# Moving two start addresses in SBUF: normed activations to 192 modulo 256, weight pieces by 128 bytes

## The reference

```python
# first block
mod = silu(c) @ w_ada[l] + b_ada[l]                     # 2048 -> 12288
h = rmsnorm(x, g_mix[l]) * (1.0 + sc1) + sh1
x = x + gt1 * hybrid_mixer(h, w_in, ..., w_out)         # pool, attention and LRU branches
h = rmsnorm(x, g_ffn[l]) * (1.0 + sc2) + sh2
x = x + gt2 * ((silu(causal_dwconv(h @ w_gate)) * (h @ w_up)) @ w_down)   # 2048 -> 5632 -> 2048
# second block, two layers
h = rmsnorm_2(x, norm_mix[l]);  proj = h @ w_in[l]      # three kinds of attention
x = x + mix @ w_o[l]
h = rmsnorm_2(x, norm_mlp[l])
u = relu(h @ w_up[l]);  x = x + (u * u) @ w_down[l]     # 2048 -> 8192 -> 2048
```

## The kernel before, in words

| tile | role in the matmuls | mod 256 | mod 512 |
|---|---|---|---|
| xT | none | 128 | 128 |
| h_hl (hi and lo, 16384 bytes apart) | moving | 128 | 128 |
| raw/w_lo and w_hi, slot 0 | stationary | 128 | 128 |
| slot 1 | stationary | 0 | 256 |
| slot 2 | stationary | 128 | 384 |
| slot 3 | stationary | 0 | 0 |
| sq, ident, ones, cols, mod | small matmuls, columns | 128 | 128 |
| act_hi, act_lo | moving | 192 | 448 |

## Time and profile before

### The profile page before, as it was taken

How to read it: one execution, slowest core, us unless ns; L and a number is a source line. 1 busy time by engine, 2 the same in 40 slices (tenths; PEclk the granted TensorE clock), 3 DMA queues, 4 the chain that set the end, 5 groups by cost and what they waited for, 6 DMA issues and landing times.

```text
span 3693.4 us, 59737 instructions
## 1 busy us (share of the span) xinstructions
PE 3377.6 (91%) x25150; PEld 3178.7 (86%) x25150; DVE 2343.3 (63%) x2598; ACT 1431.1 (39%) x1408; POOL 158.2 (4%) x292
## 2 busy tenths in 40 slices
PE   3497996999999988999999999998898999999997
PEld 3486886999999978877899999998787889999997
DVE  6777778756555566557655665666556756566655
ACT  1133433343443434344444443443343534344343
POOL 2111111100000000002000000000001000000000
PEclk9998998999999999999999999999999999999999
DMA  9687766755555543334455555554334455555553
GB/s 321 225 274 268 270 235 244 249 184 190 183 184 190 182 159 116 125 100 140 160 189 187 193 184 191 188 187 148 115 107 128 143 171 184 191 188 187 192 186 122
DMA packets 320586, 681.63 MB, mean 185 GB/s; under 512 B 14608, under 2 KB 21460, under 8 KB 320004
## 3 DMA queue, kind: packets, MB, share of 16 engines
q1 hardware_dynamic: 283440, 560.11, 45.4%
q0 software_dynamic: 31232, 109.07, 8.5%
q10 hardware_dynamic: 5780, 10.53, 0.9%
HBM read 677.47 MB, written 7.94 MB: 186 GB/s over the span
## 4 chain that ended last, share of the span: by engine, by line
PE 80%; DVE 11%; DMA 5%; issue 3%; ACT 2%; ACTq 0%; POOL 0%; POOLq 0%; DVEq 0%; SPq 0%
PE G L598 47%; PE Dn L598 31%; DMA ada_raw<-in_w_ada 3%; DVE ada_acc L1164 2%; DVE w_lo L1063 2%; PE Dn L601 1%; DMA raw<-in_w_in 1%; DVE sq L1099 1%; ACT w_hi L1792 1%; DVE negmax L1391 0%; DVE xT L1418 0%; DVE xT L1629 0%; DVE h_hl L1637 0%; DVE sq L1615 0%; DVE s_sb L1388 0%
## 5 line engine op out<-in xcount | busy, mean ns | idle before, releaser
L598 PE MATMUL G<-h_hl,w_hi 128*128 128x256 f32 (+1 forms) x9472 | 2109.2, 312 | 62.5 <-DVE w_lo L1063 21.2
L598 PEld LDWEIGHTS G<-h_hl,w_hi 128*128 128x128 f32 x9472 | 1567.6, 194 | 169.2 <-issue 32.4
L598 PE MATMUL G<-h_hl,w_lo 128*128 128x256 f32 x5760 | 1641.8, 285 | 0.0
L1063 DVE TENSOR_TENSOR w_lo<-raw,w_hi 128x2048 fp32r<-128x2048 f32 (+2 forms) x536 | 1218.7, 2274 | 599.5 <-ACT w_hi L1792 596.8
L1792 ACT CAST w_hi<-raw 128x2048 fp32r<-128x2048 f32 (+2 forms) x536 | 1015.5, 1896 | 1419.7 <-DMA raw<-in_w_up 395.6
L598 PEld LDWEIGHTS G<-h_hl,w_lo 128*128 128x128 f32 x5760 | 1110.8, 193 | 0.0
L598 PE MATMUL Dn<-act_hi,w_hi 128*128 128x256 f32 x2752 | 763.5, 277 | 7.3 <-DVE act_lo L1500 7.3
L598 PE MATMUL Dn<-act_lo,w_hi 128*128 128x256 f32 x2752 | 762.5, 277 | 0.0
L598 PE MATMUL Dn<-act_hi,w_lo 128*128 128x256 f32 x2752 | 762.5, 277 | 0.0
L598 PEld LDWEIGHTS Dn<-act_hi,w_hi 128*128 128x128 f32 x2752 | 517.4, 188 | 9.1 <-DVE act_lo L1500 7.9
L598 PEld LDWEIGHTS Dn<-act_hi,w_lo 128*128 128x128 f32 x2752 | 517.6, 188 | 0.0
(11 more groups left out here) (193 smaller groups left out, 1607.7 us busy)
## 6 DMA issues: line engine op xcount, KB each, us to landing
raw<-in_w_up SPq DMA_DIRECT2D x128, 1024.0 KB, 5.4
raw<-in_w_down SPq DMA_DIRECT2D x128, 1024.0 KB, 5.0
ada_raw<-in_w_ada POOLq DMA_DIRECT2D x192, 512.0 KB, 5.7
raw<-in_w_in SPq DMA_DIRECT2D x88, 1024.0 KB, 5.2
raw<-in_w_ffn_gate SPq DMA_DIRECT2D x44, 1024.0 KB, 5.0
raw<-in_w_ffn_up SPq DMA_DIRECT2D x44, 1024.0 KB, 5.0
raw<-in_w_ffn_down SPq DMA_DIRECT2D x44, 1024.0 KB, 5.0
raw<-in_w_o SPq DMA_DIRECT2D x32, 1024.0 KB, 5.0
```

What stands on the lines that cost most here:

```text
L598: return nc.tensor.matmul(o, lhsT, rhs, start=start, stop=stop, skip_group_check=True)
L1063: v.tensor_tensor(w_lo[j][:, 0:m], raw[j][:, 0:PIECE_K * n], w_hi[j][:, 0:m], ALU.subtract).then_inc(lo_done, 1)
```

## The change

The two 64-byte tiles `rs_v` and `rs_y` (scratch of the reciprocal root) are declared earlier: one between `xT` and `h_hl`, one between `h_hl` and the weight slots. No instruction is added, removed or reordered.

```diff
         xT = sb("xT", [P, KT, T])
+        rs_v = sb("rs_v", [P, 16])
         h_hl = sb("h_hl", [P, 2, KT, T], F32R)
         h_hi, h_lo = h_hl[:, 0, :, :], h_hl[:, 1, :, :]
+        rs_y = sb("rs_y", [P, 16])
         over = ExitStack()
         raw = [sb(f"raw{i}", [P, PIECE_K * 520], F32, over) for i in range(SLOTS)]
...
         amod = sb("amod", [P, 2, KT])
-        rs_v = sb("rs_v", [P, 16])
-        rs_y = sb("rs_y", [P, 16])
         rs_z = sb("rs_z", [P, 16])
```

## The result

The changed kernel takes 3661.3 us, the median of four runs (3657.5 to 3667.2); the kernel before, beside it on the same chip, 3694.2. The ratio of the two is 0.9909, with a 95% interval of 0.9894 to 0.9924: faster by 33 us or 0.9%, where the forecast said 83.6 us and a time between 3585 and 3645.

The account below looks back on a forecast made before the run. The matmul stream alone was taken to bound the feed-forward loops, its pace set by tile start addresses. 27.1 + 6.8 + 24.0 + 25.7 = 83.6 us off 3694.6 gave 3611.0 us, range 3585 to 3645.

Parts of the forecast that it names:

- (a): First feed-forward part, 11 groups: all 12 pieces at 5.44 us, group 65.28 instead of 67.75 us, saving 27.1 us.
- (b): Down slot 0 in the second block, 32 groups: from 5.65 to 5.44 us, saving 6.8 us.
- (c): Up in the second block, pairs of 512 and 256 columns: from 351.7 to 340 ns each, saving 24.0 us.
- Rival 1: Residues modulo 512 decide; a quarter of all pieces stay at 117.7 ns; 56.7 us saved, 3638 us; chance 0.15.
- (0,192): Stationary residue 0, moving 192, modulo 256: slot 0 of gate and up after the change, forecast at 113.3 ns.
- Rival 3: Second block's up: the pair does not follow its parts' pace; 59.6 us saved, 3635 us; chance 0.17.
- (d): Projections and attention of all three layers, 6960 matmuls on h_hl: saving between 10.4 and 41.1 us, middle 25.7 taken.
- (e): Some 900 small matmuls through ident, ones and sq, residues 128 to 0: 0 taken, 6 us to either side.
- Rival 2: No effect: G, its accumulation or h_hl's place slows gate, so 5.75 and 5.70 only exchange slots; 3694 us; chance 0.08.
- Rival 4: Slower: h at 192 locks every slot to gate's 119.8 ns, pairs 359.4; 3710 us; chance 0.05.

Follow-up runs that it names:

- The second execution of the changed kernel: The changed kernel run again with nothing altered, beside two other versions on the same chip: 3661.6 us, ratio 0.9908 to the kernel before.
- the probe: Whole computation left out; matmul streams alone over eight stationary and eight moving tile residues, all combinations: 113.3 to 120.0 ns a matmul, pairs 346.7 to 353.3.
- the split version of before: Kernel before, h_hl still at 128, each 512-column matmul of the second block's up projection written as two of 256: 3705.8 us, ratio 1.003.
- the all-192 kernel: Changed kernel's h and act at 192, all eight weight slots at 0: with pairs 3683.9 us; with pairs split 3642.5 us, six runs 3620.4 to 3661.0.

## Why the prediction was right and wrong, step by step

**What bounds the kernel, and that addresses matter:** right. Not an instruction was added, TensorE stayed busy in all but 2.5 us of each loop, and the loops shortened with the pace alone.

**(a) First feed-forward part, 27.1 us:** 22.7 measured. The size of a group, 65.28 us, came exactly. 4.5 us were counted for gate and up of groups 0 and 1 and 1.6 came. 13 of these 16 pieces run at 113 ns and TensorE's busy time falls by 3.5 us, but its idle time grows from 8.1 to 10.1 us: this part is not bound by the matmuls alone, and I counted it as if it were. In the loop 1.5 us less came than the groups give. Its last down group waits 2.5 us for `act_lo` in both kernels; after this wait the granted clock is 0.74 and 0.91 in the two stretches of 5 us from 1320 us on, where it was 1.00 before, that is some 1.7 us of time lost once. The second execution of the changed kernel has 3.4 us at the lower clock in this loop too, the version with h alone moved has none, so it comes and goes.

**(b) Down slot 0 in the second block, 6.8 us:** right, 5.65 to 5.46 us, 32 x 0.19 = 6.1, which the loops hold together with the loss of (c). The reading that this slot is slow by its history holds: with h alone moved it has the residues of before and runs at 113.3 ns in the first block's loop. Rival 1 is refuted by the profile after (gate slot 1, with the difference 192 modulo 512, runs at 113.3 ns). But the mechanism was only half told. In the second block of that same version slots 0 to 2 are slow, so the weights' shift was needed there. And the probe shows that the entry chooses between two paces at one pair of residues, where I had taken (0,192) for fast "in a usual group"; it was fast in all the loops of the changed kernel, which no row assured.

**(c) Pairs, 24.0 us:** this is the step that failed, and the largest miss: -3 us instead (32 x -0.09), 27 off. I argued that the present pair costs three present matmuls (351.7 and 3 x 117.2) and would follow its parts to 340. But 117.2 is only 351.7 / 3 and stands in no row. The parts at that address are gate's 118.7 and 119.8, which give 357.6 (3 x 119.2), as the split version of before then showed. So the pair was already faster than its parts, and the earlier trace rows said so. What the runs show in place of this step: the pair has a pace of its own for each difference. The probe has it at 353.3 at 192, its slowest. Rival 3, with 0.17, was the case. Only with the pair split does the forecast's 21.76 us a group come, by another edit.

**(d) Projections and attention, 25.7 us:** 9.5 measured, just under the lower end of 10.4, but not for the reason from which that end was worked out. The stream did get nearly as fast as the middle supposed. Taken over the matmuls that follow one another directly at the full clock, the mean distance of starts in these stages falls from 119.2 to 116.0 ns, stretches at 113.3 mixed with stretches at 117.7, and 3.2 x 6960 is 22 us. What failed is that the waits and the clock were put at nothing beyond this: TensorE's idle time in these stages grows from 134 to 141 us, and its time at the lower clock from 129 to 142 us, 11 us more of it busy and so some 5 us lost. In the second execution mixer 1's projections were 7 us shorter and the later stages of (d) longer by as much; idle time (142 us), time at the lower clock (143) and the 9.5 us below before came out alike. Why faster matmuls meet the lower clock more often was not looked into.

**(e) Small matmuls, 0:** not measured by itself; nothing in the differences asks for more. VectorE and ScalarE (2344.0 and 1432.7 us busy) are unchanged within 2 us, and DMA went from 186 to 192 GB/s in the first loop without becoming a bound, as reckoned.

In sum: 83.6, less 4.4 in (a), less 28.1 in (b) and (c), which together gave 2.7 of 30.8, less 16.2 in (d), leaves the 34.9 us of the stages. The step that failed first is (c), the pair priced by its parts; the second is (d), where faster matmuls were to cost nothing in waits and clock. The sign was right, and the saving at the upper end of the range was too large: 3645 held rival 3 alone (3635) but not rival 3 together with the lower end of (d), 3651, and the shortfall of (a) on top. Rival 2 falls: gate is not at 5.75 and 5.70. The rule in the Trainium skill, SBUF — State Buffer, section "SBUF: two separate sides", that the other engine ports never wait for anyone may be true of engines against each other; of TensorE's own two reads the probe shows 113.3 to 120.0 ns by nothing but where the tiles start, with the other engines idle but for a mark of ScalarE's between blocks. Rival 4 had a grain of truth, pairs that grow (by 1.4 ns, not the 3.3 from which it would decide the sign), but not at gate.

**What stays open.** Which part of SBUF or of TensorE's reading the two operands collide in, and why differences 64 and 192 have two paces, were not found. Nor was a rule for which of the two a piece takes: the step from 64 to 192 frees down in the changed kernel and before, but not always, and neither a fast nor a slow piece hands on its pace for certain. Pairs at difference 32 or 160 together with gate and down at 192 would need h in two places and were not tried. Nor was it found what lets one execution of the all-192 kernel enter its loop slow and another not.

## What to carry to other kernels

When a stream of matmuls bounds a kernel, divide the time between the first matmuls of two pieces by their count, for each combination of tiles, and compare: paces that differ by 5% at equal shapes can come from the addresses, and moving one tile tells. Here it paid to place the moving tile 192 and 64 bytes above the stationary ones modulo 256, alternating, and to write 256-column matmuls there; the change with split pairs, 3635 us against 3694, was the best steady version. Do not price a form that the trace doesn't show at the sum of its parts; measure it in a probe, or carry both ends and say which way the rows point. And where the bound engine also waits, price the waits and the clock: here 22 us of faster matmuls came out as 9.5.

## What was not expected of the hardware

- The pace of a 256-column matmul depends on where the tiles start, by their difference modulo 256: 113.3 to 120.0 ns, and 346.7 to 353.3 for a pair of 512 and 256 columns, with no difference good for both.
- A 512-column matmul can be slower than two of 256 columns with one more weight load: 353.1 against 340.0 ns for the same work.
- At differences 64 and 192 the stream has two paces, 113.3 and 117.8 ns. Which one it takes depends on what ran before, and a fast piece ahead is no help: in the probe three of eight blocks at 192 were fast behind a piece at 113.3 ns, and seven of eight behind one at 120.0. With all differences at 192 one pace then lasted a whole loop of 658.5 us, and six runs of this kernel lay 41 us apart.
- Where TensorE also waits, more than half of what faster matmuls won was lost again: 22 us won and 9.5 kept, with idle time up from 134 to 141 us and time at the lower clock from 129 to 142.
- Small waits cost clock, not in every execution: 3.84 us of waiting was followed by 10 us at a granted clock of 0.60, and a wait of 2.5 us by a lower clock after and by none before.
